# Giving GpSimd a fifth of the subtractions of a mixture-of-experts stage, and loading its first tiles later

## The chip, the cores and the metric

The kernel runs on one core of a Trainium2 chip, as one launch. The metric is the device time of that launch in microseconds (us), the median of repeated runs. Engines are named as in the profile: PE (TensorE matmuls) with PEld (its weight loads), ACT (ScalarE), DVE (VectorE), POOL (GpSimd), SP (SyncE, which here issues DMAs).

## The reference

The whole computation is two transformer blocks on 512 tokens of width 1024, in float32. The change concerns only the last feed-forward layer, a mixture of 8 experts over 256 tokens, two experts for each token:

```python
def swiglu(u, wg, wu, wd):
    return (jax.nn.silu(u @ wg) * (u @ wu)) @ wd

def moe_swiglu(u, w_router, wg, wu, wd):
    ...
    logits = (xf @ w_router).astype(F32)
    vals, idx = lax.top_k(logits, TOP_K_EXPERTS)
    w = jax.nn.softmax(vals, axis=-1)
    gate = jnp.sum(jax.nn.one_hot(idx, N_EXPERTS, dtype=F32) * w[..., None], axis=1)
    y = jnp.zeros_like(xf)
    for e in range(N_EXPERTS):
        y = y + gate[:, e:e + 1].astype(xf.dtype) * swiglu(xf, wg[e], wu[e], wd[e])
```

For each expert the gate and up matrices are 1024 x 3584 and the down matrix is 3584 x 1024.

## The kernel before

Everything ahead of the experts is a sequence of stages that the change leaves alone. `router_stage` picks two experts for each token. `seat_stage` gathers up to 128 tokens for each expert into `route.seated` with matmuls. `moe_stage` then computes the experts one after another. A second pass through both stages stands under a condition (an expert with over 128 tokens) and does not run here.

PE multiplies in the type fp32r, so each float32 operand is split in two: `hi`, its leading part, and `lo`, the rest. A product takes three matmul passes: x_hi w_hi, x_lo w_hi, x_hi w_lo. `moe_stage` streams the weights in **units** of 128 rows. An expert has 92: first 64 **up** units of 896 columns, in 4 groups of 16 (8 gate units, then 8 lift units, for a quarter of the hidden columns), then 28 **down** units of 1024 columns. For each unit u:

- SP loads its tile (mostly two units, 896 KB or 1 MB) into one of 6 raw slots. Three slots are the tensor `raw_ring`, two lie in `H`, one in the constants' level masks (`const`). A slot is loaded anew once the last unit of its old tile has been subtracted (`parted`).
- ACT copies the unit to `weights_hi` (L3321, counter `cut`). There are 4 buffers, so it waits until PE has used unit u-4.
- DVE computes `weights_lo` = raw - hi for the whole width (L3360, counter `parted`).
- PE waits for `parted` and does 6 matmuls (L3297), then counts `used`.

Between units each engine has other work at fixed places, in program order. In each group, at u % 16 == 11 ACT applies Silu to the gate rows and copies the turned rows to `hidden_hi` (L3329, L3336); at u % 16 == 3 of the next group DVE multiplies the rows (L3370), and at u % 16 == 12 it subtracts for `hidden_lo` (L3377), each as two instructions with one input in PSUM. PE transposes rows at u % 16 == 6 (L3256). The output of the expert before is copied at u = 3 and scattered and added from u = 5 to 16 (L3268, L3354).

At an expert's start ACT splits the seated tokens into `expert_x_hi` (L3316) after its last cut of the expert before, and POOL subtracts for `expert_x_lo` (L3243, 1024 columns), its only instruction in an expert. PE waits for it before unit 0.

`seat_stage` also loads the first 4 tiles of expert 0 (`MOE_EARLY`): they go to the three slots of `raw_ring` and to the masks, which that stage does not use. `moe_stage` starts with tile 4.

Of the kernel before, what the change touches and what calls it, by code (L numbers as in the profile page):

```python
# [2968 lines left out]
MOE_SLOTS, MOE_EARLY, MOE_GROUPS = 6, 4, 4  # L2969


class Raw:


    def __init__(self, core, st, route, turn):
        masks = CONST_AT["level0_0"][0]
        assert CONST_AT[f"level{LEVELS - 1}_1"][1] - masks == 2 * D
        in_H = st.H[:].rearrange("p k t -> p (k t)").rearrange("p (s n) -> p s n", s=2)
        self.at = [*(route.raw_ring[:, i] for i in range(MOE_SLOTS - 3)), st.const[:, masks:masks + 2 * D], in_H[:, 0], in_H[:, 1]]
        self.landed = [core.counter(f"moe_raw{s}_landed_{turn}", True) for s in range(MOE_SLOTS)]  # L2980
        self.w_up = [st.A[n][0].rearrange("e (k p) n -> p e k n", p=P) for n in ("moe_w_gate_2", "moe_w_up_2")]

    def load_up(self, sp, e, t):

        wide = FE // MOE_GROUPS
        g, m, k0 = t // DC, t % DC // 4, t % 4 * 2
        src = self.w_up[m][:, ds(e, 1), k0:k0 + 2, g * wide:(g + 1) * wide]
        at = self.at[t % MOE_SLOTS][:, 0:2 * wide].rearrange("p (k n) -> p k n", n=wide)
        sp.dma_start(at, src.rearrange("p e k n -> p (e k) n")).then_inc(self.landed[t % MOE_SLOTS].sem, 16)
# [159 lines left out]
def moe_stage(core, st, route, turn):  # L3149
# [27 lines left out]
    width_of = lambda u: WIDE if u < UP else D  # L3177

    with ExitStack() as ctx, core.engines_block() as block:
        raw_tiles = Raw(core, st, route, turn)  # L3180
# [16 lines left out]
        names = ("cut", "parted", "used", "x_cut", "x_ready", "gated", "rows_ready", "turned", "h_cut", "h_ready",  # L3197
                 "act_y_copied", "dve_y_copied", "scattered", "y_added")
        (cut, parted, used, x_cut, x_ready, gated, rows_ready, turned, h_cut, h_ready,
         act_y_copied, dve_y_copied, scattered, y_added) = (core.counter("moe_" + n) for n in names)  # L3200
# [358 lines left out]
```

## Time and profile before

| | |
|---|---|
| median of 3 runs | 3990.3 us (3982.96 to 3992.85) |
| the profiled execution's own time | 3990.3 us |
| its span, first to last instruction | 3988.3 us |
| PE, PEld busy over the span | 85%, 66% |
| DVE, ACT, POOL busy over the span | 63%, 37%, 9% |
| mean granted PE clock, as a share of full speed | 0.903 |
| the expert stage, first cut to the end of the last subtraction | 2938 to 3952 us |

The expert stage is the last quarter of the span; the shares over the whole span mix it with stages that have other limits, so the stage is read by itself. A timeline row gives the start, the duration, engine, line, operation, tile written <- tiles read, and in brackets the idle time of that engine before it and what ended it. Rows marked xN merge N instructions that follow one another.

### The profile page before, as it was taken

What the parts mean: (1) busy time and instruction counts of PE and PEld (TensorE: products, weight loads), DVE (VectorE), ACT (ScalarE), POOL (GpSimd) and SP (SyncE); (2) the same over time, 40 slices, a digit from 0 to 9 for tenths busy, and PEclk for the clock granted to TensorE, in tenths of its full rate; (3) what the DMA queues carried; (4) which work ended last, traced back from release to release, by engine and by line L of the source; (5) the groups of instructions that cost most, each with busy time, mean ns of one, the idle gap of its engine ahead of it and who ended that gap; (6) DMA issues with size and microseconds to landing.
All of it is one profiled execution on the core that took longest, in us unless ns stands there. A gap on an engine that the chain in (4) does not pass through costs nothing. (4 is left out here: it accounts for less than half of the span.)

```text
span 3988.3 us, 67458 instructions
## 1 busy us (share of the span) xinstructions
PE 3379.2 (85%) x25980; PEld 2632.9 (66%) x25980; DVE 2523.6 (63%) x4138; ACT 1478.8 (37%) x2693; POOL 346.1 (9%) x338
## 2 busy tenths in 40 slices
PE   5897876999778798779866798778689999999997
PEld 2644555874365687668764687665568888888886
DVE  2436657889666445669346351146458888888887
ACT  1123312110202665311011200214257777777775
POOL 0000003442100221021000020000000000000000
PEclk8998987999888899989986899865789999999998
DMA  7310012328222000168520495120159999999995
GB/s 307 95 56 1 1 42 79 95 92 256 79 88 60 3 5 4 36 223 277 192 89 7 143 320 175 68 87 3 43 211 356 338 355 343 350 351 344 346 348 205
DMA packets 296869, 645.55 MB, mean 162 GB/s; under 512 B 24989, under 2 KB 155145, under 8 KB 296521
## 3 DMA queue, kind: packets, MB, share of 16 engines
q1 hardware_dynamic: 272889, 556.32, 39.8%
q0 software_dynamic: 23040, 83.90, 6.1%
q8 instruction: 158, 2.59, 0.3%
q10 hardware_dynamic: 720, 2.23, 0.1%
q14 instruction: 62, 0.51, 0.0%
HBM read 641.34 MB, written 1.05 MB: 161 GB/s over the span
## 5 line engine op out<-in xcount | busy, mean ns | idle before, releaser
L3360 DVE TENSOR_TENSOR weights_lo<-raw_ring,weights_hi 128x896 fp32r<-128x896 f32 (+1 forms) x376 | 425.6, 1157 | 77.2 <-ACT weights_hi L3321 66.7
L3321 ACT ACTIVATE weights_hi<-raw_ring 128x896 fp32r<-128x896 f32 (+1 forms) x376 | 364.2, 985 | 122.3 <-PE bank_pair L3297 122.1
L323 PE MATMUL bank_pair<-H,ring_up 128*128 128x256 f32 x1408 | 311.0, 383 | 25.4 <-DMA ring_up<-in_ffn_w_gate 9.2
L3297 PE MATMUL bank_pair<-weights_hi,expert_x_hi 128*128 128x512 f32 (+1 forms) x1024 | 306.4, 380 | 21.9 <-DVE weights_lo L3360 21.9
L323 PEld LDWEIGHTS bank_pair<-H,ring_up 128*128 128x128 f32 x1408 | 269.1, 192 | 66.9 <-DVE conv L1760 11.0
L3297 PE MATMUL bank_pair<-weights_lo,expert_x_hi 128*128 128x512 f32 (+1 forms) x1024 | 294.2, 368 | 0.0
L3297 PE MATMUL bank_pair<-weights_hi,expert_x_lo 128*128 128x512 f32 (+1 forms) x1024 | 294.1, 368 | 0.0
L323 PE MATMUL bank_pair<-x_hi,ring_hi_in 128*128 128x512 f32 (+1 forms) x576 | 210.5, 365 | 94.7 <-DVE ring_lo_in L298 82.0
L3360 DVE TENSOR_TENSOR weights_lo<-H,weights_hi 128x896 fp32r<-128x896 f32 (+1 forms) x240 | 263.7, 1132 | 32.3 <-ACT weights_hi L3321 26.0
L3321 ACT ACTIVATE weights_hi<-H 128x896 fp32r<-128x896 f32 (+1 forms) x240 | 235.2, 993 | 77.9 <-PE bank_pair L3297 77.9
L323 PE MATMUL bank_pair<-ffn_h,ring_down 128*128 128x512 f32 (+1 forms) x704 | 232.2, 492 | 24.1 <-DMA ring_down<-in_ffn_w_down 19.9
L3297 PEld LDWEIGHTS bank_pair<-weights_hi,expert_x_hi 128*128 128x128 f32 x1024 | 181.7, 188 | 59.7 <-DVE weights_lo L3360 32.1
L323 PEld LDWEIGHTS bank_pair<-ffn_h,ring_down 128*128 128x128 f32 x704 | 134.8, 193 | 121.2 <-issue 88.1
L323 PE MATMUL bank_pair<-x_lo,ring_hi_in 128*128 128x512 f32 (+1 forms) x576 | 206.5, 358 | 0.0
L323 PE MATMUL bank_pair<-x_hi,ring_lo_in 128*128 128x512 f32 (+1 forms) x576 | 206.2, 358 | 0.0
L3297 PEld LDWEIGHTS bank_pair<-weights_hi,expert_x_lo 128*128 128x128 f32 x1024 | 186.7, 188 | 24.4
L3297 PEld LDWEIGHTS bank_pair<-weights_lo,expert_x_hi 128*128 128x128 f32 x1024 | 186.1, 188 | 24.7
L323 PEld LDWEIGHTS bank_pair<-x_hi,ring_hi_in 128*128 128x128 f32 x576 | 114.1, 198 | 117.6 <-DVE ring_lo_in L298 85.0
L1760 DVE SCALAR_TENSOR_TENSOR conv<-bank_pair,taps,conv 128x189 f32<-128x189 f32 (+2 forms) x352 | 151.0, 431 | 24.8 <-ACT conv L1791 13.1
L579 DVE SCALAR_TENSOR_TENSOR mod_sums_ada<-mod_ring_ada,act,mod_sums_ada 128x512 f32 (+1 forms) x192 | 144.1, 751 | 21.0 <-DMA mod_ring_ada<-in_w_ada 15.1
L323 PE MATMUL bank_pair<-x_hi,ring_hi_up 128*128 128x512 f32 x352 | 138.1, 392 | 19.8 <-DVE x_lo L355 19.8
L3297 PE MATMUL bank_pair<-weights_hi,hidden_hi 128*128 128x512 f32 x448 | 138.9, 391 | 0.0
(628 smaller groups left out, 6636.5 us busy)
## 6 DMA issues: line engine op xcount, KB each, us to landing
raw_ring<-in_moe_w_gate SPq DMA_DIRECT2D x72, 896.0 KB, 6.6
raw_ring<-in_moe_w_up SPq DMA_DIRECT2D x64, 896.0 KB, 6.3
ring_up<-in_ffn_w_up SPq DMA_DIRECT2D x110, 512.0 KB, 4.1
mod_ring_ada<-in_w_ada POOLq DMA_DIRECT2D x96, 512.0 KB, 6.5
raw_ring<-in_moe_w_down SPq DMA_DIRECT2D x48, 1024.0 KB, 7.0
H<-in_moe_w_up SPq DMA_DIRECT2D x48, 896.0 KB, 7.1
H<-in_moe_w_down SPq DMA_DIRECT2D x32, 1024.0 KB, 7.3
H<-in_moe_w_gate SPq DMA_DIRECT2D x32, 896.0 KB, 6.3
```

The costliest lines, as they stand in the source:

```text
L323: ins = self.core.nc.tensor.matmul(self.banks[o][:, 0:moving.shape[1]], lhs, moving, start=(s == self.first[o] and k == 0 and i == 0), sto ...
L579: self.core.nc.vector.scalar_tensor_tensor(at, self.ring[:, s, k % self.PART], self.st.act[:, k, c:c + 1], at, ALU.mult, ALU.add).then_inc ...
L1760: ins = nc.vector.scalar_tensor_tensor(yg[:, rows[0], rows[1]], xg[:, from_[0], from_[1]], taps[:, o, w:w + 1], yg[:, rows[0], rows[1]], A ...
L3297: ins = nc.tensor.matmul(banks[half][:, 0:b - a], x, w[:, a:b], start=start and i == 0, stop=stop and i == 2)
L3321: nc.scalar.activation(hi[:, u % CUTS, 0:n].bitcast(F32R), raw_part(u), ACT.Copy).then_inc(cut.sem, 1)
L3360: nc.vector.tensor_tensor(lo[:, u % CUTS, 0:n].bitcast(F32R), raw_part(u)[:, 0:n], hi[:, u % CUTS, 0:n], ALU.subtract).then_inc(parted.sem, 1)
```

## The change

1. The subtraction of a unit is divided by columns: DVE takes columns 0 to 703 of an up unit and 0 to 799 of a down unit; POOL takes the other 192 or 224. `parted` becomes two counters, `dve_parted` and `pool_parted`.
2. PE waits for both counters ahead of a unit. SP waits for both ahead of a tile, with an increment of a counter that nobody reads (`sp_passed`) between the two waits.
3. `seat_stage` loads nothing any more. SP loads all tiles of expert 0 in `moe_stage`, as one loop over 8 experts in place of a first round and a loop over 7. `raw_ring` is allocated in `moe_stage`.
4. The slots have another order: the masks are slot 5 and the halves of `H` are slots 3 and 4.

```diff
-        raw = Raw(core, st, route, turn)
-
-        @block.sync
-        def _(sp):
-            for t in range(MOE_EARLY):
-                raw.load_up(sp, 0, t)
...
+    dve_columns = lambda u: 704 if u < UP else 800
...
+        raw = [*(raw_ring[:, i] for i in range(SLOTS - 3)), raw_in_H[:, 0], raw_in_H[:, 1], st.const[:, masks:masks + 2 * D]]
...
         def _(sp):
-            def body(e, first):
-                for t in range(MOE_EARLY if first else 0, TILES):
-                    wait_parted(sp, e if t >= SLOTS else e - 1, units_of[t - SLOTS][-1])
+            with sp.Fori(0, EXPERTS) as e:
+                for t in range(TILES):
+                    u = units_of[t - SLOTS][-1]
+                    wait_pool_parted(sp, e if t >= SLOTS else e - 1, u)
+                    sp.sem_inc(sp_passed.sem, 1)
+                    wait_dve_parted(sp, e if t >= SLOTS else e - 1, u)
...
         def _(pool):
+            pool.sem_inc(pool_parted.sem, UNITS)
             with pool.Fori(0, EXPERTS) as e:
...
                 nc.gpsimd.tensor_tensor(x_lo[:].bitcast(F32R), seated, x_hi[:], ALU.subtract).then_inc(x_ready.sem, 1)
+                for u in range(UNITS):
+                    pool.wait_ge(cut.sem, cut.at(e * UNITS + u + 1))
+                    wait_used(pool, e if u >= CUTS else e - 1, (u - CUTS) % UNITS)
+                    at = slice(dve_columns(u), width_of(u))
+                    nc.gpsimd.tensor_tensor(lo[:, u % CUTS, at].bitcast(F32R), raw_part(u)[:, at], hi[:, u % CUTS, at], ALU.subtract).then_inc(pool_parted.sem, 1)
...
-                    wait_parted(pe, e, u)
+                    wait_pool_parted(pe, e, u)
+                    wait_dve_parted(pe, e, u)
...
             def body(e, first):
                 for u in range(UNITS):
-                    n = width_of(u)
+                    n = dve_columns(u)
                     dve.wait_ge(cut.sem, cut.at(e * UNITS + u + 1))
-                    nc.vector.tensor_tensor(lo[:, u % CUTS, 0:n].bitcast(F32R), raw_part(u)[:, 0:n], hi[:, u % CUTS, 0:n], ALU.subtract).then_inc(parted.sem, 1)
+                    nc.vector.tensor_tensor(lo[:, u % CUTS, 0:n].bitcast(F32R), raw_part(u)[:, 0:n], hi[:, u % CUTS, 0:n], ALU.subtract).then_inc(dve_parted.sem, 1)
```

## Rows read from the trace of the kernel before

**Rows 1.** Windows: length, busy time of each engine, PE clock, DMA share, GB/s.

```profile
2895.50:2908.00 12.50, 7.16 (x21) 4.91 (x22) 10.32 (x38) 0.00 (x0) 0.00 (x0) 0.51 0.77 294
2938.50:2945.20 6.70, 3.33 (x9) 2.97 (x10) 5.63 (x4) 3.74 (x5) 2.28 (x1) 0.50 0.89 301
2945.30:3953.00 1007.70, 992.19 (x4736) 847.98 (x4736) 889.89 (x895) 774.56 (x875) 16.80 (x7) 1.00 0.94 344
```

**Rows 2.** Waits from 2960 to 3940 us: total us, times, longest.

```profile
ACT weights_hi L3321 <- PE bank_pair L3297: 225.8, 585, 1.1
...
PE bank_pair L3297 <- DVE weights_lo L3360: 15.1, 31, 0.6
```

**Rows 3.** Timeline, unit pace: ACT cuts in the up and down phases.

```profile
3352.43 0.96 ACT L3321 ACTIVATE weights_hi<-raw_ring 128x896 fp32r<-128x896 f32 x1 [0.28 <-PE bank_pair L3297]
3353.67 0.96 ACT L3321 ACTIVATE weights_hi<-raw_ring 128x896 fp32r<-128x896 f32 x1 [0.29 <-PE bank_pair L3297]
...
3410.29 1.06 ACT L3321 ACTIVATE weights_hi<-H 128x1024 fp32r<-128x1024 f32 x1 [0.30 <-PE bank_pair L3297]
3411.65 1.07 ACT L3321 ACTIVATE weights_hi<-H 128x1024 fp32r<-128x1024 f32 x1 [0.29 <-PE bank_pair L3297]
```

**Rows 4.** Timeline of the end of a group of 16 units.

```profile
3358.23 1.81 ACT L3321 ACTIVATE weights_hi<-raw_ring 128x896 fp32r<-128x896 f32 x2
...
3359.23 1.09 DVE L3360 TENSOR_TENSOR weights_lo<-raw_ring,weights_hi 128x896 fp32r<-128x896 f32 x1 [1.48 <-ACT weights_hi L3321]
...
3360.24 1.15 DVE L3377 TENSOR_TENSOR hidden_lo<-bank_pair,hidden_hi 128x512 fp32r<-128x512 f32 x2
...
3361.30 1.08 DVE L3360 TENSOR_TENSOR weights_lo<-raw_ring,weights_hi 128x896 fp32r<-128x896 f32 x1
...
3362.44 0.68 PE L3297 MATMUL bank_pair<-weights_hi,expert_x_hi 128*128 128x512 f32 x2 [0.58 <-DVE weights_lo L3360]
```

**Rows 5.** Timeline of an expert's end and the next one's start; one DVE subtraction.

```profile
3317.80 1.77 ACT L3321 ACTIVATE weights_hi<-raw_ring 128x896 fp32r<-128x896 f32 x2
...
3318.07 2.40 POOL L3243 TENSOR_TENSOR expert_x_lo<-seated,expert_x_hi 128x1024 fp32r<-128x1024 f32 x1 [124.37 <-ACT expert_x_hi L3316]
...
3321.47 0.68 PE L3297 MATMUL bank_pair<-weights_hi,expert_x_hi 128*128 128x512 f32 x2 [0.19 <-DVE weights_lo L3360]
...
L3360 DVE TENSOR_TENSOR weights_lo<-raw_ring,weights_hi x1: 2651/2651/2651, 3318.8 to 3318.8; 128x896 fp32r<-128x896 f32 x1
```

**Rows 6.** Norm stage at 1061 us: POOL and DVE side by side; ns min/median/max.

```profile
L901 POOL TENSOR_TENSOR norm_work<-Y x2: 1029/1256/1483, 1061.5 to 1062.5; 128x512 f32<-128x512 f32 x2
...
L873 DVE TENSOR_TENSOR norm_work<-Y x4: 677/1102/1578, 1061.5 to 1065.1; 128x512 f32<-128x512 f32 x4
```

**Rows 7.** Groups of POOL by shape: 1024 and 256 columns.

```profile
L3243 POOL TENSOR_TENSOR expert_x_lo<-seated,expert_x_hi 128x1024 fp32r<-128x1024 f32 x8 | 19.2, 2394 | 943.8 <-ACT expert_x_hi L3316 943.8
...
L2296 POOL TENSOR_TENSOR kappa<-rw_k,kappa 128x256 f32<-128x256 f32 x16 | 11.7, 730 | 1.3
```

**Rows 8.** Group of DVE by shape: the 1024-column subtraction.

```profile
L3360 DVE TENSOR_TENSOR weights_lo<-H,weights_hi 128x1024 fp32r<-128x1024 f32 x78 | 91.8, 1219 | 1.9
```

**Rows 9.** Start of the expert stage; time to landing of its first DMA.

```profile
2938.14 3.45 ACT L3321 ACTIVATE weights_hi<-raw_ring 128x896 fp32r<-128x896 f32 x4
...
2941.88 1.09 PE L3297 MATMUL bank_pair<-weights_hi,expert_x_hi 128*128 128x512 f32 x2 [6.34 <-DVE weights_lo L3360]
...
L2989 SPq DMA_DIRECT2D H<-in_moe_w_up x1: 368/368/368, 2937.1 to 2937.1; - x1
...
DMA to landing us min/median/max: 5.0/5.0/5.0
```

**Rows 10.** First tile of the fifth expert: landing, and ACT's first use.

```profile
L2989 SPq DMA_DIRECT2D raw_ring<-in_moe_w_gate x1: 389/389/389, 3436.7 to 3436.7; - x1
...
DMA to landing us min/median/max: 6.5/6.5/6.5
...
3444.30 1.77 ACT L3321 ACTIVATE weights_hi<-raw_ring 128x896 fp32r<-128x896 f32 x2
```

More of the change, by code:

```diff
@@ L2966, in _ @@
                     nc.scalar.activation(dst[:, :, 0:N_CMP], bank[:, 0:KV_HEADS * N_CMP].rearrange("p (g n) -> p g n", g=KV_HEADS), ACT.Copy)
[L2969 to L2989, printed above, removed]
 class Route:
@@ L3146, in _, with moe_stage @@
                 stored.count(nc.scalar.activation(route.seated[:, g * 4:(g + 1) * 4, k], core.bank(n % 4).rearrange("p (e s) -> p e s", e=4), ACT.Copy))
-def moe_stage(core, st, route, turn):
+def moe_stage(core, st, route):
     nc, A = core.nc, st.A
-    GROUPS = MOE_GROUPS
+    GROUPS = 4
     WIDE = FE // GROUPS
@@ L3177, in moe_stage @@
     width_of = lambda u: WIDE if u < UP else D
+    dve_columns = lambda u: 704 if u < UP else 800
     with ExitStack() as ctx, core.engines_block() as block:
-        raw_tiles = Raw(core, st, route, turn)
-        raw, landed = raw_tiles.at, raw_tiles.landed
+        raw_ring = core.sb("raw_ring", [P, SLOTS - 3, 2 * D], ctx=ctx)
+        raw_in_H = st.H[:].rearrange("p k t -> p (k t)").rearrange("p (s n) -> p s n", s=2)
+        masks = CONST_AT["level0_0"][0]
+        assert CONST_AT[f"level{LEVELS - 1}_1"][1] - masks == 2 * D
+        raw = [*(raw_ring[:, i] for i in range(SLOTS - 3)), raw_in_H[:, 0], raw_in_H[:, 1], st.const[:, masks:masks + 2 * D]]
         hi, lo = (core.sb(f"weights_{n}", [P, CUTS, D], ctx=ctx) for n in ("hi", "lo"))
@@ L3196, in like @@
             return bank[half][:, 0:b - a].rearrange("p (c t) -> p c t", c=rows[half].shape[1])
[L3197 to L3200, printed above, removed]
+        landed = [core.counter(f"moe_raw{s}_landed") for s in range(SLOTS)]
+        names = ("cut", "dve_parted", "pool_parted", "used", "x_cut", "x_ready", "gated", "rows_ready", "turned", "h_cut", "h_ready",
+                 "act_y_copied", "dve_y_copied", "scattered", "y_added", "sp_passed")
+        (cut, dve_parted, pool_parted, used, x_cut, x_ready, gated, rows_ready, turned, h_cut, h_ready,
+         act_y_copied, dve_y_copied, scattered, y_added, sp_passed) = (core.counter("moe_" + n) for n in names)
         GATE, LIFT = (core.bank(0), core.bank(1)), (core.bank(2), core.bank(3))
         TURN, DOWN = (core.bank(4), core.bank(5)), (core.bank(6), core.bank(7))
+        w_up = [A[n][0].rearrange("e (k p) n -> p e k n", p=P) for n in ("moe_w_gate_2", "moe_w_up_2")]
         w_down = A["moe_w_down_2"][0].rearrange("e (k p) n -> p e k n", p=P)
@@ L3207, in raw_part, with wait_dve_parted, wait_pool_parted @@
             return raw[t % SLOTS][:, j * width_of(u):(j + 1) * width_of(u)]
-        def wait_parted(eng, e, u):
-            eng.wait_ge(parted.sem, parted.at(UNITS + e * UNITS + u + 1))
+        def wait_dve_parted(eng, e, u):
+            eng.wait_ge(dve_parted.sem, dve_parted.at(UNITS + e * UNITS + u + 1))
+        def wait_pool_parted(eng, e, u):
+            eng.wait_ge(pool_parted.sem, pool_parted.at(UNITS + e * UNITS + u + 1))
         def wait_used(eng, e, u):
@@ L3232, in body @@
                         src = w_down[:, ds(e, 1), c:c + n, :]
-                        at = raw[t % SLOTS][:, 0:n * D].rearrange("p (k n) -> p k n", n=D)
-                        sp.dma_start(at, src.rearrange("p e k n -> p (e k) n")).then_inc(landed[t % SLOTS].sem, 16)
-            rounds(sp, EXPERTS, body)
+                        at = at[:, 0:n * D]
+                    sp.dma_start(at.rearrange("p (k n) -> p k n", n=src.shape[3]), src.rearrange("p e k n -> p (e k) n")).then_inc(landed[t % SLOTS].sem, 16)
         @block.gpsimd
         def _(pool):
+            pool.sem_inc(pool_parted.sem, UNITS)
             with pool.Fori(0, EXPERTS) as e:
@@ L3385, in moe_stage @@
             c.n += 16 * LAPS * EXPERTS
-        for c, n in ((cut, UNITS * EXPERTS), (parted, UNITS * (EXPERTS + 1)), (used, UNITS * (EXPERTS + 1)),
+        for c, n in ((cut, UNITS * EXPERTS), (dve_parted, UNITS * (EXPERTS + 1)), (pool_parted, UNITS * (EXPERTS + 1)), (used, UNITS * (EXPERTS + 1)),
                      (x_cut, EXPERTS), (x_ready, EXPERTS), (gated, GROUPS * EXPERTS), (rows_ready, GROUPS * EXPERTS), (turned, 1 + GROUPS * EXPERTS),
                      (h_cut, GROUPS * EXPERTS), (h_ready, 1 + GROUPS * EXPERTS), (act_y_copied, EXPERTS), (dve_y_copied, EXPERTS),
+                     (sp_passed, EXPERTS * TILES),
                      (scattered, 4 * EXPERTS), (y_added, 4 * (EXPERTS + 1))):
```

14 lines of the change are left out of this document (8 added, 6 removed).

## The prediction

> **What bounds the kernel now.** I read the windows of the expert stage first. From 2945 to 3953 us PE is busy 992 of 1008 us at the granted clock 1.00, DVE 890, ACT 775, the DMA engines 0.94 of the time, POOL 17 us [rows 1]. Four numbers near full don't say which sets the pace; the list of waits does. ACT waits for PE to free a buffer 585 times, and PE waits for DVE's subtraction 31 times, 15.1 us in all [rows 2]. So PE sets the pace, and DVE, though 88% busy, costs about 15 us. The timeline gives PE's pace through ACT, which starts each cut as PE frees a buffer: 1.24 us for an up unit, 1.36 us for a down unit [rows 3]. An expert takes 126.5 us (first cuts at 3317.80 and 3444.30) [rows 5, 10].
>
> The 31 waits are of two kinds, by count 3 x 8 group ends and 7 expert starts. At a group's end ACT's extra work delays the cut of unit 28; DVE subtracts it, does `hidden_lo` (1.15 us) and only then unit 29, from 3361.30 to 3362.38, and PE goes on at 3362.44 after 0.58 us idle [rows 4]. At an expert's start POOL's `expert_x_lo` runs from 3318.07 to 3320.47, DVE's first subtraction, begun at 3318.8, takes 2.65 us instead of 1.09 and ends at 3321.42, and PE starts 0.05 us later, after 0.19 us idle [rows 4, 5].
>
> **POOL and DVE exclude each other here.** That 2.65 us is the row on which most depends. DVE ended 0.95 us after POOL did, whenever it had started. The norm stage shows the same for 512 columns: POOL's first instruction took 1.03 us, DVE's longest 1.58 against 0.68 alone, that is 0.55 after POOL, and POOL's next took 1.48 instead of 1.03, since it waited in turn [rows 6]. The waiting instruction has done its start-up by then (0.68 - 0.55 = 0.13 us, and 1.09 - 0.95 = 0.14). `hidden_lo` and the row products read PSUM with one operand; I take it that they don't join this queue.
>
> **The change, part by part.**
>
> *The shared resource per unit.* DVE holds it 0.95 us for 896 columns and 0.55 for 512, 1.04 ns a column: 0.75 us for 704 and 0.85 for 800 [rows 5, 6]. POOL alone takes 2.39 us for 1024 columns and 0.73 for 256, 2.17 ns a column [rows 7], so 0.59 us for 192 and 0.66 for 224. Its hidden start-up is between 0.10 (1.48 - 0.55 = 0.93 against 1.03, [rows 6]) and 0.17 (what the line through rows 7 leaves at no columns), so it holds 0.42 to 0.49 and 0.49 to 0.56 us. Together: 1.17 to 1.24 us for an up unit against PE's 1.24, and 1.34 to 1.41 for a down unit against PE's 1.36. I take 1.20 and 1.36. Before, DVE alone needed 1.09 and 1.22 [rows 4, 8], less where they overlap. The change thus lowers DVE's instruction and raises what a unit needs of the shared resource; it fits under PE, but with nothing to spare in the down phase. A backlog made there stays.
>
> *Group ends, 24 of them.* Unit 28 is ready after 0.14 + 0.75 + 0.45 = 1.34 us instead of 1.09, which is covered by the wait for unit 29. DVE reaches unit 29 about 0.2 us earlier, at 3361.1. By then POOL holds the resource for unit 30 (cut at about 3360.9: units 28 and 29 are cut by 3358.23 + 1.81 = 3360.04, the next one 0.85 later [rows 4]) until about 3361.55; DVE then ends at 3362.30 instead of 3362.38. Gain 0.08 x 24 = 1.9 us. Bounds: a gain of 0.2 each if POOL is not in between, a loss of 0.25 if it comes in ahead once more: -5 to +6 us.
>
> *Expert starts, 7 of them.* POOL now has unit 91 ahead of `expert_x_lo`. Unit 91 is cut some 0.85 us before ACT's first cut of the next expert (only `expert_x_hi` lies between), at about 3316.95 [rows 5]. Without a backlog both engines are through with it at 3316.95 + 0.15 + 1.36 = 3318.45; `expert_x_lo` holds from 3318.6 for 2.25 us to 3320.85, DVE's unit 0 ends at 3321.6 and POOL's, new, at 3322.05. PE starts 0.6 us later than at 3321.47. If unit 91 is late by 1 us, or DVE's unit 0 gets in ahead of `expert_x_lo` (they ask at nearly the same time), POOL's unit 0 comes behind DVE's unit 1: 3321.9 + 0.75 + 0.45 = 3323.1, 1.6 us late. With both it is 2.2 us. All of PE's matmuls are queued behind its new wait for POOL, and PE has no slack afterwards to win this back, so it lengthens the run. I take 1.5, near the second case, since the down phase clears no backlog: 7 x 1.5 = 10.5 us; bounds 4 and 15.
>
> *Down phase.* DVE comes into it behind, and the row products (two instructions, as long as `hidden_lo`, 1.15 us) stand at unit 67. POOL can only fill some 0.9 us of such a pause, as it runs out of cut units. Followed unit by unit with 1.34 us, unit 68 is 0.25 us late for PE and unit 77 up to 0.15 us. I take 0.35 x 8 = 2.8 us; bounds 0 and 8.
>
> *The early tiles.* SP issued four tiles in `seat_stage` (the DMA engines were busy 0.77 of 2895 to 2908 us); nothing waited for them there, so taking them out gives nothing. Before, the first cut was at 2938.14 and PE started at 2941.88 [rows 9]. Now the first tile is issued at 2937.1 and lands 5.0 us later, as the first one issued there does [rows 9]: 2942.1. Cut 0.96, DVE 0.89, POOL 0.45 more: PE starts at 2944.4, 2.5 us later. Later tiles come faster than PE uses them at first. PE ran its first microseconds at the granted clock 0.50 [rows 1], the level of 1.2 GHz; idle 2.5 us longer it may stay there a little longer, and each microsecond there does half the work of one at full clock: 0.8 us more (0 to 2). Sum 3.3, bounds 2.5 and 4.5.
>
> *SP's two waits.* The counter increment and the second wait delay a tile by a fraction of an issue (0.37 us, [rows 9]); a backlog of subtractions delays it by up to 1 us. The thinnest place is an expert's first tile: issued at 3436.7, landed at 3443.2, used at 3444.30 [rows 10], a margin of 1.1 us, and behind it the cut may be 2 us late, because `expert_x_lo` holds DVE up anyway. What is queued behind SP's waits is the next tiles alone. Costed at nothing; without that cover a backlog of 1 us would cost up to 1 us an expert. The order of the slots moves no byte: nothing. POOL's loop over 92 units has no other work queued behind it but `expert_x_lo`, counted above.
>
> *The sum.* 3.3 + 10.5 + 2.8 - 1.9 = 14.7 us. The profiled execution took 3990.3 us (span 3988.3), which is also the median: 4005.0 us, 0.37% slower.
>
> **A rule that says more.** The trace has the waiting DVE instruction finish 0.95 us after POOL and not 1.09, so its start-up was not held [rows 4, 5]. The Trainium skill, "SBUF — State Buffer", section "Who interferes with whom", says that the shared pair of ports goes to whichever of DVE and GpSimd issues first, for the whole instruction. Taken at its word, with whole durations, this gives the fourth rival's time; with the held times the rule and the rows agree, and the sum stands.
>
> **The rivals.**
>
> *1. They run side by side when POOL's instruction is this short (8%).* Then units 28 and 29 are each 0.2 us earlier, 24 x 0.4 = 9.6 us, expert starts gain 0.1 each, and the early tiles cost 3.3: 3990.3 - 9.6 - 0.7 + 3.3 = 3983 us, not slower. It decides only if POOL's hold is nought; rows 5 and 6 are against it, though both are for POOL instructions of 512 columns and more.
>
> *2. Everything but the start is hidden (14%).* The pauses of PE (transposes, scatters) clear the backlog, and unit 91 is never late: 3.3 + 7 x 0.3 - 1.9 = 3.5: about 3994 us. For it: 1.20 is under 1.24. Against: DVE has 1.15 us pauses in every group.
>
> *3. The resource is the bound (17%).* If POOL holds over 0.49 us for 192 columns or 0.51 for 224, each unit is longer than PE's. At 0.05 us over for an up unit and 0.08 for a down unit an expert takes 64 x 0.05 + 28 x 0.08 = 5.4 us more, 43 us in all with the pauses of PE giving some back: 4020 to 4060 us.
>
> *4. Whole instructions exclude each other (4%).* 0.89 + 0.59 = 1.48 for an up unit, 0.99 + 0.66 = 1.65 for a down unit: 64 x 0.24 + 28 x 0.29 = 23.5 us an expert, 188 us in all: 4178 us. Against it: the 0.95 and 0.55 us above.
>
> *5. Late tiles (2%).* The margin of 1.1 us falls below nothing at 7 starts and the cover is gone: some 7 us on top, 4012 us.
>
> **How the numbers follow.** The forecast has 55%, with a range of its own of 3996 to 4016 us. A measurement here tells about 0.3%, 12 us, from no change: above 4002.3 is slower. Two thirds of the forecast (37%), rivals 3, 4 and 5 (23%) lie there: 60%. The rest of the forecast, rival 2 and most of rival 1 are within it: 36%. Faster keeps 4%, for a rival 1 that also takes away the remaining group waits. For 8 in 10 the range runs from 3988 (rival 1 left out) to 4035 (half of rival 3 and rival 4 left out).
>
> **What would show it.** POOL subtractions of 0.56 to 0.66 us alone and about 1.3 when they wait; DVE's at 0.89 alone and up to 1.35 behind POOL; PE waiting for POOL by name; PE's first matmul near 2944.4; first cuts of successive experts some 128.2 us apart, against 126.5; units of 1.24 and 1.36 us in between. It is wrong if the distance stays at 126.5 (rival 2), falls (rival 1), or if the units themselves lengthen (rivals 3 and 4), and if ACT waits for a DMA at an expert's start (rival 5).

## The result and the profile after

The changed kernel takes 4046.1 us (median of 4 runs, 4043.88 to 4056.86) against 3991.6 us for the kernel before in the same comparison. The ratio is 1.0144, 95% interval 1.0118 to 1.0170: slower, and above the predicted range. The profiled execution of after took 4066.35 us. Its expert stage begins 20.8 us later than that of before (first cut 2958.9 against 2938.1); 4.4 us of this belong to the change, the rest to stages that the change leaves alone and that vary between executions. So the expert stage is read by itself, and mainly one number of it: the distance from an expert's first cut to the next one's, a mean over experts 2 to 7. It is 126.79 us before and 134.83 after, 8.0 us more where the terms of the sum gave 1.6 (1.5 + 0.35 - 3 x 0.08).

The windows of after: the first from 7.2 us behind the stage's first cut to its end, as in [rows 1], the second behind one expert's start:

```profile
2966.10:4029.00 1062.90, 1012.37 (x4726) 849.56 (x4725) 932.58 (x894) 773.80 (x874) 801.81 (x739) 0.98 0.91 328
3499.90:3504.00 4.10, 4.09 (x11) 3.62 (x12) 0.50 (x2) 0.95 (x1) 1.86 (x4) 0.50 0.99 372
```

PE's busy time is longer than in [rows 1] and the clock no longer 1.00; POOL went from 17 to 802 us. The second row shows why the clock fell: 4.1 us at 0.50, the level of 1.2 GHz, behind an idle PE. The waits of the stage, against [rows 2]:

```profile
ACT weights_hi L3312 <- PE bank_pair L3288: 263.7, 573, 5.8
...
PE bank_pair L3288 <- POOL weights_lo L3233: 39.5, 7, 6.8
POOL expert_x_lo L3228 <- issue: 32.6, 7, 5.3
...
ACT weights_hi L3312 <- DMA raw_ring<-in_moe_w_gate: 20.4, 13, 3.5
...
PE bank_pair L3288 <- DVE weights_lo L3351: 7.3, 25, 0.5
```

PE's waits for DVE halved, from 15.1 to 7.3 us. In their place stand 7 waits for POOL of 5.6 us each: the seven expert starts. POOL itself, ahead of each `expert_x_lo`, stood 32.6 us in all waiting for nothing that the profile shows ("issue"), and ACT waited 13 times for a tile.

Between the starts the units kept their pace. ACT's cuts in both phases, POOL's subtraction of an up unit alone, and DVE's of a down unit, against [rows 3]:

```profile
3395.60 0.95 ACT L3312 ACTIVATE weights_hi<-raw_ring 128x896 fp32r<-128x896 f32 x1 [0.28 <-PE bank_pair L3288]
3396.84 0.96 ACT L3312 ACTIVATE weights_hi<-raw_ring 128x896 fp32r<-128x896 f32 x1 [0.29 <-PE bank_pair L3288]
...
3485.01 1.06 ACT L3312 ACTIVATE weights_hi<-H 128x1024 fp32r<-128x1024 f32 x1 [0.30 <-PE bank_pair L3288]
3486.37 1.07 ACT L3312 ACTIVATE weights_hi<-H 128x1024 fp32r<-128x1024 f32 x1 [0.30 <-PE bank_pair L3288]
...
3390.51 0.60 POOL L3233 TENSOR_TENSOR weights_lo<-H,weights_hi 128x192 fp32r<-128x192 f32 x1 [0.64 <-ACT weights_hi L3312]
...
3485.60 1.45 DVE L3351 TENSOR_TENSOR weights_lo<-raw_ring,weights_hi 128x800 fp32r<-128x800 f32 x1
```

1.24 us and 1.36 us, as before. POOL's 192 columns take 0.60 us alone (0.59 predicted), DVE's 800 take 1.45 us beside POOL (up to 1.35 predicted).

The timeline of the boundary where the fifth expert begins, against [rows 5] and [rows 10]:

```profile
3480.64 0.33 SPq L3219 DMA_DIRECT2D const<-in_moe_w_down  x1
3485.81 2.90 SPq L3219 DMA_DIRECT2D raw_ring<-in_moe_w_gate  x3
...
3488.70 1.05 ACT L3307 ACTIVATE expert_x_hi<-seated 128x1024 fp32r x1
...
3488.96 1.40 POOL L3233 TENSOR_TENSOR weights_lo<-const,weights_hi 128x224 fp32r<-128x224 f32 x1
...
3490.99 1.80 ACT L3312 ACTIVATE weights_hi<-raw_ring 128x896 fp32r<-128x896 f32 x2 [1.24 <-DMA raw_ring<-in_moe_w_gate]
...
3494.51 1.79 ACT L3312 ACTIVATE weights_hi<-raw_ring 128x896 fp32r<-128x896 f32 x2 [1.72 <-DMA raw_ring<-in_moe_w_gate]
3495.49 3.84 DVE L3351 TENSOR_TENSOR weights_lo<-raw_ring,weights_hi 128x704 fp32r<-128x704 f32 x2 [1.78 <-ACT weights_hi L3312]
3495.63 2.94 POOL L3228 TENSOR_TENSOR expert_x_lo<-seated,expert_x_hi 128x1024 fp32r<-128x1024 f32 x1 [5.28 <-issue]
...
3498.54 2.88 POOL L3233 TENSOR_TENSOR weights_lo<-raw_ring,weights_hi 128x192 fp32r<-128x192 f32 x4
...
3499.91 1.11 PE L3288 MATMUL bank_pair<-weights_hi,expert_x_hi 128*128 128x512 f32 x2 [6.77 <-POOL weights_lo L3233]
```

POOL ends unit 91 at 3490.36. `expert_x_hi` has been ready since 3489.75, and yet `expert_x_lo` starts at 3495.63: 5.28 us in which POOL waits for no one. PE needs it, and POOL's part of unit 0 behind it, and starts at 3499.91 after 6.77 us idle (5.3 to 5.9 at the other six starts, 0.19 in [rows 5]). SP has a hole too: no tile is issued between 3480.64 and 3485.81, and so the first tiles of the new expert land late; ACT waits 1.24 and 1.72 us for them. In both streams the hole stands exactly behind the jump from the end of the loop's body to its start. Measured from the end of the branch instruction to the next instruction:

| engine | kernel before | after, at its 7 jumps |
|---|---|---|
| POOL | 0.11 us | 5.4 to 6.3 us |
| SP | 0.20 us | 4.0 to 4.3 us |
| DVE, ACT | 0.2 us | 0.2 us |

The page's list of DMA queues has a row that answers to it, the queue that brings instructions. First after, then before:

```profile
q14 instruction: 136, 1.11, 0.1%
```

```profile
q14 instruction: 62, 0.51, 0.0%
```

74 packets more in an execution. When they come says more than how many. From 3300 to 3900 us, a stretch that holds no stage but this one, the kernel before has no packet of this queue, and after has 46:

```profile
q14 instruction: 46, 0.38, 0.2%
```

Most come in bursts behind SP's and POOL's jumps: 7 lie between 3481 and 3500 us, around the boundary shown above. Instructions are being loaded again.

### The profile page after: what moved, and what is told of

Read it like the earlier page. It is cut to its first block and busy times, and to the rows that moved or that the text cites. A ratio compares the mean times of both kernels' runs of the same rounds, so it can differ in the third digit from the quotient of the medians.

```text
span 4064.4 us, 70956 instructions
## 1 busy us (share of the span) xinstructions
PE 3414.1 (84%) x25980; PEld 2642.5 (65%) x25980; DVE 2568.1 (63%) x4138; ACT 1478.0 (36%) x2693; POOL 1137.4 (28%) x1074
## 3 DMA queue, kind: packets, MB, share of 16 engines
HBM read 641.34 MB, written 1.05 MB: 158 GB/s over the span
## 5 line engine op out<-in xcount | busy, mean ns | idle before, releaser
L3351 DVE TENSOR_TENSOR weights_lo<-raw_ring,weights_hi 128x704 fp32r<-128x704 f32 (+1 forms) x376 | 438.7, 1205 | 101.2 <-ACT weights_hi L3312 100.5
L3233 POOL TENSOR_TENSOR weights_lo<-raw_ring,weights_hi 128x192 fp32r<-128x192 f32 (+1 forms) x376 | 399.8, 1075 | 135.5 <-ACT weights_hi L3312 108.7
L3288 PE MATMUL bank_pair<-weights_hi,expert_x_hi 128*128 128x512 f32 (+1 forms) x1024 | 314.9, 389 | 57.2 <-POOL weights_lo L3233 49.6
L3351 DVE TENSOR_TENSOR weights_lo<-H,weights_hi 128x704 fp32r<-128x704 f32 (+1 forms) x240 | 283.1, 1216 | 26.5 <-ACT weights_hi L3312 26.2
L3233 POOL TENSOR_TENSOR weights_lo<-H,weights_hi 128x192 fp32r<-128x192 f32 (+1 forms) x240 | 259.1, 1089 | 68.1 <-ACT weights_hi L3312 57.0
L901 POOL TENSOR_TENSOR norm_work<-X 128x512 f32<-128x512 f32 x7 | 8.2, 1170 | 771.1 <-SPq L196 771.1
```

Source lines behind the costliest of these rows:

```text
L901: nc.gpsimd.tensor_tensor(work[0][:, q], jobs[0].x(q), jobs[0].x(q), ALU.mult).then_inc(pool_squared.sem, 1)
L3233: nc.gpsimd.tensor_tensor(lo[:, u % CUTS, at].bitcast(F32R), raw_part(u)[:, at], hi[:, u % CUTS, at], ALU.subtract).then_inc(pool_parted.s ...
L3288: ins = nc.tensor.matmul(banks[half][:, 0:b - a], x, w[:, a:b], start=start and i == 0, stop=stop and i == 2)
L3351: nc.vector.tensor_tensor(lo[:, u % CUTS, 0:n].bitcast(F32R), raw_part(u)[:, 0:n], hi[:, u % CUTS, 0:n], ALU.subtract).then_inc(dve_parted ...
```

## The experiments

What had to be told apart: (a) how much of the 8.0 us is this reloading, (b) what makes a loop reload, its length or something else, (c) whether POOL and DVE exclude each other with their held times, as predicted, (d) what the start and the group ends are worth. The loop's body, in instructions of one expert:

| | POOL | SP | DVE | ACT |
|---|---|---|---|---|
| before | 6 | 176 | 224 | 219 |
| after | 282 | 269 | 224 | 251 |

All distances below are of one profiled execution each, as the mean of six; the ratios are of 4 to 10 runs beside the kernel before. They are not the quotients of the two pooled medians, which differ from them by up to 0.2% (`short_both`: ratio 1.0044, medians 4021.9 and 3997.0 us, quotient 1.0062). A difference of 0.2% or less between two kernels is therefore read from the trace and not from the ratios.

### 1. Shorter loops: POOL alone, then POOL and SP

`short_pool` drops POOL's wait for the buffer of `weights_lo`, which PE's use has cleared anyway once ACT has cut the unit (190 instructions left). `short_both` also merges SP's waits at ten pairs of tiles (249 left).

```diff
                     pool.wait_ge(cut.sem, cut.at(e * UNITS + u + 1))
-                    wait_used(pool, e if u >= CUTS else e - 1, (u - CUTS) % UNITS)
...
+        AHEAD = (8, 11, 14, 17, 20, 23, 26, 29, 32, 35)
...
-                    sp.sem_inc(sp_passed.sem, 1)
-                    wait_dve_parted(sp, e if t >= SLOTS else e - 1, u)
+                    if t - 1 not in AHEAD:
+                        sp.sem_inc(sp_passed.sem, 1)
+                        wait_dve_parted(sp, e if t >= SLOTS else e - 1, units_of[t + 1 - SLOTS][-1] if t in AHEAD else u)
```

> The changed kernel without POOL's wait for `used` ahead of each subtraction (the wait for `cut` implies it); POOL does the same 93 subtractions an expert with about 190 instead of 282 instructions in its loop's body. Theory A (a loop's branch back stalls an engine for about 5.5 us when the body is longer than the engine holds, somewhere between 251 and 271 instructions by the traces so far): the gap behind POOL's branch falls from 5.4 to 6.3 us to about 0.1, and the first cuts of successive experts stand 128 to 130 us apart instead of 134.8; the time falls from 4046 to 4005 to 4015 us. Theory B (POOL and DVE together are the bound because they exclude each other): the waits taken away hold already, so nothing changes: 4046 us and 134.8. Theory C (the cost lies in SP's late tiles): POOL's gap may go, but the distance stays above 132.

> As short_pool, and SP's body is cut from 271 to 251 instructions too: at 10 of the 48 tiles SP waits for DVE's subtraction of one tile further on and leaves out the wait and the increment at the next tile. Theory A: the gap behind SP's branch falls from 4.1 us to 0.2, ACT no longer waits for a tile at an expert's start, and the distance of experts is 127.5 to 129 us, the time 4000 to 4008 us, what my prediction of 4005 had costed without any branch. Theory B: 134.8 and 4046. Theory C: only this kernel, and not short_pool, falls below 132.

Measured: `short_pool` 1.0045 [1.0029, 1.0061], distance 129.08 us; POOL's hole is gone (0.0 us), SP's is still there (4.0 to 5.0). `short_both` 1.0044 [1.0027, 1.0062], distance 129.02; both are gone. The same boundary in `short_both`:

```profile
3473.15 1.05 ACT L3309 ACTIVATE expert_x_hi<-seated 128x1024 fp32r x1
...
3473.38 1.42 POOL L3235 TENSOR_TENSOR weights_lo<-const,weights_hi 128x224 fp32r<-128x224 f32 x1
...
3474.09 1.78 ACT L3314 ACTIVATE weights_hi<-raw_ring 128x896 fp32r<-128x896 f32 x2
...
3474.76 3.15 POOL L3231 TENSOR_TENSOR expert_x_lo<-seated,expert_x_hi 128x1024 fp32r<-128x1024 f32 x1
...
3475.57 5.49 DVE L3353 TENSOR_TENSOR weights_lo<-raw_ring,weights_hi 128x704 fp32r<-128x704 f32 x3
...
3479.23 0.67 PE L3290 MATMUL bank_pair<-weights_hi,expert_x_hi 128*128 128x512 f32 x2 [1.66 <-POOL weights_lo L3235]
```

`expert_x_lo` starts 0.67 us after ACT's first cut, PE 5.14 us after it (3479.23 - 3474.09); before it was 3.67 us (3321.47 - 3317.80, [rows 5]). The difference is 1.47 us. So POOL's reloading cost 5.8 us an expert, 134.83 - 129.08, and SP's hole nothing that can be told while it stood (129.08 against 129.02): in `short_pool` ACT waits 18.9 us in all for tiles, but PE has to wait for `expert_x_lo` and the subtractions behind it for as long anyway. Of the 5.8 us, 4.0 are PE's longer wait (5.64 us in the mean against 1.67). The other 1.8 are longer matmuls. From the second expert's first matmul to the eighth's, six experts, PE's busy time is 767.94 us in after and 756.71 in `short_both`, 1.87 an expert more. First after, then `short_both`:

```profile
3094.33:3903.34 809.01, 767.94 (x3577) 645.06 (x3577) 708.38 (x679) 584.24 (x660) 605.77 (x559) 0.98 0.91 327
```

```profile
3092.29:3866.36 774.07, 756.71 (x3576) 633.86 (x3577) 724.39 (x679) 584.38 (x660) 627.31 (x559) 1.00 0.91 341
```

The count of matmuls is the same and the clock is not: in `short_both` it stays at 1.00 at every one of these starts, in after it is 0.50 for 3.4 to 6.8 us around each.

### 2. Length or place: the same loops moved

A length limit would have to lie between 249 and 269. The other theory is that instructions lie in blocks with fixed borders, that two blocks are held, and that a body which touches a third must be loaded anew at each jump. `pad_dve` makes DVE's loop of the kernel before longer than any of these, by a second, needless wait at the 64 up units (288 instructions). `shift_both` takes the loops of after as they are and moves them, by 40 instructions ahead of them on POOL and on SP. `pad_dve_moved` does it the other way round: the loop of `pad_dve`, 212 instructions further on.

```diff
                     dve.wait_ge(cut.sem, cut.at(e * UNITS + u + 1))
+                    if u < 64:
+                        dve.wait_ge(cut.sem, cut.at(e * UNITS + u + 1))
```

```diff
+            for _ in range(40):
+                sp.sem_inc(shift.sem, 1)
...
+            for _ in range(40):
+                pool.sem_inc(shift.sem, 1)
```

```diff
+            for _ in range(212):
+                dve.sem_inc(shift.sem, 1)
```

> The kernel before with each of DVE's waits for `cut` in the up phase written twice: 64 more instructions that wait for nothing new, 288 instead of 224 in the body of DVE's loop, no more data and no POOL. Theory A: the gap behind DVE's branch grows from 0.23 to 4 to 6 us at each of 6 branches back and stops PE for most of it, 25 to 45 us in all: 4015 to 4035 us. Theory B: within 2 us of the kernel before, as nothing more is shared. Theory C: the same as B.

> The changed kernel with 40 increments of a counter that nobody waits for put ahead of the loop on POOL and on SP, in the stage before, where both are idle. The bodies stay 282 and 271 instructions long; only where they lie in each engine's program moves by about 42. So far bodies of 282 (POOL), 265 and 271 (SP) stalled at their branch back, but 288 (DVE) did not, so length alone (theory A) does not explain it. Theory D: an engine holds two pages of 256 instructions, and a body that touches a third is fetched again at each branch; by the positions of all loops seen, the pages would begin at about 812 and 1068, and the bodies, which began at 791 and 811, now begin at 833 and 856 and touch two. Then the gaps fall to 0.1 and 0.2 us, experts stand 129 us apart and the time is as short_both, 4005 to 4020 us. Theory A: gaps 5.4 and 4.1 us, 134.8 us, 4046 us as before.

> pad_dve (the kernel before with 64 idle waits in DVE's loop, 288 instructions, which had no gap) with 212 idle increments put ahead on DVE in the stage before, in a 26 us pause of DVE. Theory D: the body now runs from about 3867 to 4154 and holds two page starts, so the same body stalls: gap 4 to 6 us at 6 branches, 20 to 40 us in all. Theory A' (DVE does not stall at all, only POOL and SP do): gap 0.25 us and the time of pad_dve, 1.002 of the kernel before.

Measured: `pad_dve` 1.0018 [1.0002, 1.0034], distance 127.15, DVE's jump 0.25 us. A body of 288 instructions is not reloaded, so length alone is not the cause. `shift_both`: 1.0043 [1.0030, 1.0056], distance 128.86; bodies of 282 and 272 instructions, no shorter than in after, and jumps of 0.19 and 0.20 us (0.24 and 0.26 the first time). Forty instructions of nothing ahead of the loops win back 1.0%. `pad_dve_moved`: 1.0060 [1.0041, 1.0080], distance 129.55, and DVE's jump takes 5.5 to 5.8 us. Its boundary:

```profile
3465.53 1.78 ACT L3325 ACTIVATE weights_hi<-raw_ring 128x896 fp32r<-128x896 f32 x2
...
3465.80 2.41 POOL L3247 TENSOR_TENSOR expert_x_lo<-seated,expert_x_hi 128x1024 fp32r<-128x1024 f32 x1 [127.36 <-ACT expert_x_hi L3320]
...
3470.83 4.10 DVE L3366 TENSOR_TENSOR weights_lo<-raw_ring,weights_hi 128x896 fp32r<-128x896 f32 x4 [4.89 <-ACT weights_hi L3325]
...
3471.97 0.67 PE L3301 MATMUL bank_pair<-weights_hi,expert_x_hi 128*128 128x512 f32 x2 [2.95 <-DVE weights_lo L3366]
```

DVE has the cut of the next unit from 3466.5 on and starts at 3470.83, 4.89 us idle behind what the profile calls a wait for ACT; PE starts at 3471.97 after 2.95 us. At six starts PE waits 2.7 to 3.0 us; at the seventh, where DVE's first expert, which has its own code, runs on into the loop without a jump, it waits 0.26. The distances behind a jump are 131.43, 129.77, 129.73, 129.70 and 129.43 us, against 127.14 in `pad_dve`: 2.9 us a jump (the sixth distance, 127.21, has no jump ahead of it and lowers the mean to 129.55). That is less than POOL's 5.8. PE waits 2.8 us here and not 5.6, since only unit 0 is queued behind the hole, and the clock fell at only one of the six starts, the one with 131.43.

The places, counted in each engine's compiled program, fit blocks of 256 instructions whose borders lie at the same remainder in all three programs. SP's 269 and 272 are also what the traces count between two jumps (the expectations have 271 for both):

| loop | body at | borders in it | blocks | reloaded |
|---|---|---|---|---|
| after, POOL | 791 to 1072 | 814, 1070 | 3 | yes |
| after and short_pool, SP | 813 to 1081 | 814, 1070 | 3 | yes |
| short_pool, POOL | 791 to 980 | 814 | 2 | no |
| short_both, SP | 813 to 1061 | 814 | 2 | no |
| shift_both, POOL | 833 to 1114 | 1070 | 2 | no |
| shift_both, SP | 855 to 1126 | 1070 | 2 | no |
| pad_dve, DVE | 3655 to 3942 | 3886 | 2 | no |
| pad_dve_moved, DVE | 3867 to 4154 | 3886, 4142 | 3 | yes |

The borders are inferred (46 to 48 more than a multiple of 256 fits: 45 would leave SP's loop of after in two blocks, 49 POOL's), the yes and no are measured. The packets of the instruction queue agree: 136 in after, 101 in `short_pool`, 65 in `short_both`, 68 in `shift_both`, 63 in `pad_dve`, 96 in `pad_dve_moved`. From 3300 to 3900 us there are 24 in `short_pool` and 24 in `pad_dve_moved`, and none in `short_both`, `shift_both` and `pad_dve`. That is 5 packets of 8.2 KB for each jump that reloads. The Trainium skill, "Runtime: NRT & Kernel Launch", section "Instruction fetch mechanics", states the rule: an engine other than PE holds two blocks of 256 instructions, and a taken branch to a target outside them forces a fetch. The runs agree on both numbers; the price of 4.0 to 6.3 us is theirs.

### 3. How much POOL's share costs: 16, 192 and 384 columns

`narrow` and `wide_b` are `short_both` with another division of the columns.

```diff
-    dve_columns = lambda u: 704 if u < UP else 800
+    dve_columns = lambda u: 880 if u < UP else 1008
```

```diff
-    dve_columns = lambda u: 704 if u < UP else 800
+    dve_columns = lambda u: 512 if u < UP else 592
```

> short_both (no stalls behind branches) with POOL given 16 columns of each unit instead of 192 or 224, and DVE 880 or 1008. All waits and instructions are the same; only the time that POOL holds the shared access shrinks, by my estimate from 0.45 to 0.05 us, while DVE's grows from 0.75 to 0.93. If mutual exclusion makes the 2.2 us an expert that short_both still costs (129.0 against 126.8), this takes most of it back: 127 to 127.8 us. If it is the order of POOL's work (unit 91 and then unit 0 around the 1024-column subtraction) it stays above 128.5.

> short_both with the split moved the other way: POOL subtracts 384 or 432 columns, DVE 512 or 592. If the two exclude each other for the times that I worked out (2.17 ns a column for POOL, 1.04 for DVE plus nothing), a unit needs 0.83 + 0.55 = 1.38 us in the up phase and 0.94 + 0.63 = 1.57 in the down phase, more than PE's 1.24 and 1.36, so the shared access sets the pace: 64 x 1.38 + 28 x 1.57 + 2.2 = 134.5 us an expert, at least 133, and about 4055 us. If they run side by side, each alone needs 0.97 or less, and the expert stays at 127 to 129 us.

`narrow`: 1.0011 [0.9992, 1.0029], distance 127.13, within the range expected for exclusion; the order of POOL's work alone would have left it above 128.5. `wide_b`: 1.0328 [1.0303, 1.0353], distance 142.20. Two units of a down phase in `wide_b`:

```profile
3638.26 1.31 POOL L3235 TENSOR_TENSOR weights_lo<-raw_ring,weights_hi 128x432 fp32r<-128x432 f32 x1 [0.30 <-ACT weights_hi L3314]
...
3639.87 1.31 POOL L3235 TENSOR_TENSOR weights_lo<-raw_ring,weights_hi 128x432 fp32r<-128x432 f32 x1 [0.30 <-ACT weights_hi L3314]
...
3643.36 1.70 DVE L3353 TENSOR_TENSOR weights_lo<-H,weights_hi 128x592 fp32r<-128x592 f32 x1
```

POOL's starts are 1.61 us apart, the median of the phase (1.43 in an up phase), and DVE's 592 columns take 1.70 us. By the held times of the prediction a unit needs 592 x 1.04 ns = 0.62 us for DVE and 432 x 2.17 ns = 0.94 us for POOL, which may hold up to 0.07 more: 1.56 to 1.63. Whole instructions, 0.62 + 0.14 and 0.94 + 0.17, would take 1.87 us. So the two exclude each other with their held times, and POOL's is at the upper bound taken. The same bound gives 1.39 us for a down unit of the change, where DVE's subtractions in after start 1.38 us apart (median of a down phase) and PE's units 1.36.

Where in an expert the time goes is seen from ACT's cuts. The mean over six experts of the time between the cuts of two units, as the difference to the kernel before (us):

| units | what lies there | short_both | after | narrow | wide_b | group_end |
|---|---|---|---|---|---|---|
| 0 to 4 | expert start | +1.46 | +5.52 | +0.30 | +1.93 | +0.01 |
| 4 to 12 | | -0.03 | +0.79 | 0.00 | +0.83 | -0.01 |
| 12 to 27 | | 0.00 | 0.00 | 0.00 | +0.41 | 0.00 |
| 27 to 34, 43 to 50, 59 to 66 | group ends | -0.91 | -1.05 | -0.08 | +0.40 | -1.13 |
| 34 to 43, 50 to 59 | row products | +0.84 | +0.93 | +0.12 | +5.04 | +0.14 |
| 66 to 74 | row products, down phase | +0.86 | +0.85 | 0.00 | +3.16 | +0.01 |
| 74 to 92 | | 0.00 | +1.00 | 0.00 | +3.63 | 0.00 |
| all | | +2.2 | +8.0 | +0.3 | +15.4 | -1.0 |

The row products are two DVE instructions, 1.15 us, in which POOL goes on only as far as units are cut. In `wide_b` the stretches around them hold 8.2 of its 15.4 us, but only about 3 of these are the products themselves (the one long step between cuts in each of the three stretches, 1.0 to 1.1 us above its neighbours); the rest is units that are all 0.19 to 0.25 us longer. The expectation of 134.5 us missed 142.2 by 7.7: 4.3 because the units took 1.43 and 1.61 us instead of 1.38 and 1.57 (64 x 0.05 + 28 x 0.04), and 3.4 by such pauses, which it did not have.

### 4. The start of the stage

`no_early` is the kernel before without the four early tiles (SP's loop then begins at tile 0). `short_early_b` is `short_both` with them.

```diff
-        @block.sync
-        def _(sp):
-            for t in range(MOE_EARLY):
-                raw.load_up(sp, 0, t)
...
-                for t in range(MOE_EARLY if first else 0, TILES):
+                for t in range(TILES):
```

> The kernel before with only the four early tile loads taken out; nothing is shared with POOL. As costed in the prediction: PE's first matmul of the expert stage comes 2.1 to 2.5 us later and the time is 2.5 to 4.5 us longer, too little to be told from no change. If the early loads are the cause: over 15 us.

> short_both with the four early tile loads put back in the stage before. As costed, PE's first matmul of the expert stage comes about 2.5 us earlier against the start of that stage, nothing else moves (129.0 us an expert), and the ratio to the kernel before falls from 1.0044 by under 0.001. If the early loads matter more than their start (a lead that PE keeps), it falls below 1.002.

The start in `no_early` (the expert's tokens are cut at 2946.23):

```profile
2946.23 1.06 ACT L3311 ACTIVATE expert_x_hi<-seated 128x1024 fp32r<-128x1024 f32 x1 [2.76 <-PEq L3242]
...
2950.99 1.79 ACT L3316 ACTIVATE weights_hi<-raw_ring 128x896 fp32r<-128x896 f32 x2 [3.70 <-DMA raw_ring<-in_moe_w_gate]
2951.97 2.09 DVE L3355 TENSOR_TENSOR weights_lo<-raw_ring,weights_hi 128x896 fp32r<-128x896 f32 x2 [6.17 <-ACT weights_hi L3316]
...
2953.21 1.08 PE L3292 MATMUL bank_pair<-weights_hi,expert_x_hi 128*128 128x512 f32 x2 [8.62 <-DVE weights_lo L3355]
```

The same rows of after, against [rows 9]:

```profile
2958.92 1.79 ACT L3312 ACTIVATE weights_hi<-raw_ring 128x896 fp32r<-128x896 f32 x2 [4.27 <-DMA raw_ring<-in_moe_w_gate]
...
2961.34 1.09 PE L3288 MATMUL bank_pair<-weights_hi,expert_x_hi 128*128 128x512 f32 x2 [9.39 <-POOL weights_lo L3233]
```

In both ACT waits for the first tile. In `no_early` PE starts 6.98 us after `expert_x_hi` begins, against 4.70 in before: 2.3 us later. The second expert's first cut, measured from the same point, is 2.9 us later (130.00 against 127.07), and with the division of the columns 3.9 us later (`short_both` 131.77, `short_early_b` 127.89). The ratios can't show it: 1.0001 [0.9987, 1.0014] for `no_early`, and 1.0062 [1.0037, 1.0086] for `short_early_b` beside 1.0044 [1.0027, 1.0062] for `short_both`. So the 3 to 4 us are seen in the trace only; no run showed them in the time.

### 5. Using what worked: half of one unit at each group end

The one place where dividing the work gained is the group end, -0.3 us each. `group_end` is the kernel before with POOL taking columns 448 to 895 of units 29, 45 and 61 alone, while DVE does `hidden_lo`, which reads PSUM with one operand.

```diff
+    SHARED, HALF = (29, 45, 61), 448
...
+                for u in SHARED:
+                    pool.wait_ge(cut.sem, cut.at(e * UNITS + u + 1))
+                    at = slice(HALF, WIDE)
+                    nc.gpsimd.tensor_tensor(lo[:, u % CUTS, at].bitcast(F32R), raw_part(u)[:, at], hi[:, u % CUTS, at], ALU.subtract).then_inc(halved.sem, 1)
...
-                    n = width_of(u)
+                    n = HALF if u in SHARED else width_of(u)
```

> The kernel before, with POOL helping only where PE waits for DVE: at units 29, 45 and 61 of each expert POOL subtracts 448 of the 896 columns while DVE does the hidden_lo subtraction, and DVE the other 448; everything else stays. If PE's wait there is DVE's 1.09 us behind hidden_lo, and POOL can work beside hidden_lo since that reads PSUM, PE goes on about 0.45 us earlier at each of 24 places: 126.8 to 125.5 us an expert, about 10 us or 0.25% less. If hidden_lo shares with POOL after all, POOL ends late and the time is the same or longer.

Measured: 0.9971 [0.9951, 0.9992], distance 125.81, 0.98 us less than before; over 8 experts 7.8 us, or 0.2%. A group end, against [rows 4]:

```profile
3496.71 1.81 ACT L3336 ACTIVATE weights_hi<-raw_ring 128x896 fp32r<-128x896 f32 x2
...
3497.71 1.09 DVE L3375 TENSOR_TENSOR weights_lo<-raw_ring,weights_hi 128x896 fp32r<-128x896 f32 x1 [1.48 <-ACT weights_hi L3336]
...
3498.60 1.24 POOL L3256 TENSOR_TENSOR weights_lo<-raw_ring,weights_hi 128x448 fp32r<-128x448 f32 x1 [39.65 <-ACT weights_hi L3336]
3498.72 1.15 DVE L3392 TENSOR_TENSOR hidden_lo<-bank_pair,hidden_hi 128x512 fp32r<-128x512 f32 x2
...
3499.79 0.61 DVE L3375 TENSOR_TENSOR weights_lo<-raw_ring,weights_hi 128x448 fp32r<-128x448 f32 x1
...
3500.54 0.67 PE L3312 MATMUL bank_pair<-weights_hi,expert_x_hi 128*128 128x512 f32 x2 [0.20 <-DVE weights_lo L3375]
```

POOL's 448 columns run from 3498.60 to 3499.84, beside `hidden_lo`, which is as long as in [rows 4] (1.15 us). DVE's half is done at 3500.40, 3.69 us after the cut of unit 28, against 4.15 before (3362.38 - 3358.23). PE's idle time fell from 0.58 to 0.20 us. The interval lies just below 1 and the distance is shorter at each of the experts, so the gain is real but small: 0.1% by the pooled medians (3992.0 and 3995.9 us), 0.2% by the trace, 0.3% by the ratio.

## Why the prediction was wrong

**The step that failed** is the last sentence on SP's waits: "POOL's loop over 92 units has no other work queued behind it but `expert_x_lo`, counted above." The loop's own jump was costed at nothing, and with it the code that it has to hold: 282 instructions instead of 6, in three blocks. It cost 5.8 us at each of 7 starts, 40.7 us, or 1.0% (1.0144 against 1.0043 when the same loops lie in two blocks). Nothing of this was in the rows of before, whose jumps all took 0.1 to 0.3 us, but the lengths of the loops could be counted, and the rule stood in the Trainium skill. Without this term the forecast of 4005.0 us, 0.37% slower, stands beside 0.44% [0.27, 0.62] for `short_both`, and 1.6 us an expert beside 2.2. In part that is luck: two terms below are off by 0.7 and 1.35 us an expert in opposite directions. (The forecast distance of 128.2 us also started from one expert's 126.5; the mean was 126.79.)

**Expert starts.** Predicted +1.5 us each, by unit 91 or DVE's unit 0 being in the way. Measured +1.46 without the reloading. In `short_both` unit 91 was late: POOL starts it at 3473.38, ends at 3474.80, and `expert_x_lo` waits for that.

**Group ends.** Predicted -0.08 each, with bounds of -0.2 and +0.25. Measured -0.30: mis-sized, beyond the bound. The step assumed that POOL would hold the shared resource for unit 30 when DVE comes to unit 29. DVE came first. The group end in after:

```profile
3538.64 1.81 ACT L3312 ACTIVATE weights_hi<-raw_ring 128x896 fp32r<-128x896 f32 x2
...
3540.46 1.15 DVE L3368 TENSOR_TENSOR hidden_lo<-bank_pair,hidden_hi 128x512 fp32r<-128x512 f32 x2
...
3541.52 0.88 DVE L3351 TENSOR_TENSOR weights_lo<-raw_ring,weights_hi 128x704 fp32r<-128x704 f32 x1
...
3542.46 0.30 PEld L3288 LDWEIGHTS bank_pair<-weights_hi,expert_x_hi 128*128 128x128 f32 x2 [0.23 <-DVE weights_lo L3351]
...
3541.51 1.35 POOL L3233 TENSOR_TENSOR weights_lo<-H,weights_hi 128x192 fp32r<-128x192 f32 x1
```

Both ask for it within 0.01 us. DVE's unit 29 takes 0.88 us, its time alone, and POOL's unit 30 takes 1.35 instead of 0.59. PE loads the weights of unit 29 3.8 us after the cut of unit 28, against 4.2 in [rows 4].

**Row products.** Predicted +0.35 an expert, at unit 67 alone. Measured +0.86 there, and +0.84 at units 35 and 51 together, for which the prediction has no term. The delay comes at once and is not won back, since PE sets the pace: in `short_both` the step to ACT's cut of unit 72, which waits for PE's unit 68, is 0.65 us longer than before, where the prediction found 0.25, and the steps to the cuts of units 40 and 56 are 0.44 and 0.40 longer. The 0.25 was followed with 1.34 us for a down unit, the lower end of the prediction's own 1.34 to 1.41; DVE's starts are 1.38 apart. The two mis-sized terms nearly cancel: -0.91 + 1.70 = +0.8, against -0.24 + 0.35 = +0.1.

**The units.** Right: 1.24 and 1.36 us between them, POOL 0.60 alone.

**The start.** 3.3 us predicted, 2.9 and 3.9 measured in the trace.

**SP's waits.** "Costed at nothing" holds for the waits, though not by the cover named: SP's 93 further instructions made its loop reload, the tiles came 4 us late, and PE did not feel it only because `expert_x_lo` was later still.

**The rivals.** 1 (side by side) is refuted by `narrow` and `wide_b`: the time grows with POOL's columns. 2 (only the start) by the +2.2 us an expert of `short_both`. 3 (the resource is the bound) gave a time that holds the measured one, 4020 to 4060 us, by a cause that is all but absent. Its condition is met in the down phase (1.38 us against PE's 1.36), but the units that ACT's cuts show stay at 1.24 and 1.36, except for 0.01 to 0.03 us each at units 68 to 73 of `short_both`. 4 (whole instructions exclude each other, the cited rule taken at its word) is refuted by units of 1.36 us, and by 1.61 in `wide_b`, where it gives 1.87; here the measurement decides. 5 (late tiles) happened and cost nothing.

What stays open: where exactly the blocks' borders come from, and why POOL's jump takes longer than SP's with as many packets.

## What to carry to other kernels

Ahead of moving work into a loop, count the instructions of its body, waits and increments included, on each engine: one of up to 256 lies in at most two blocks wherever it stands (none of 176 to 251 stalled here), a longer one (269 to 288) stalled at each jump or not by its place, and then 40 needless instructions ahead of it, or a wait less in each step, are worth more than the arithmetic. In a trace, look for idle time put down to nothing ("issue") at the first instruction of a loop, and compare the packets of the instruction queue. Where POOL and DVE take turns, give POOL pieces that run while DVE reads PSUM, and leave it out of the steady stretches.

## What was not expected of the hardware

- A jump back to code that is no longer held costs 5.4 to 6.3 us on POOL, 4.0 to 4.3 (5.0 in `short_pool`) on SP, and 5.5 to 5.8 on DVE, and moves 5 packets of 8.2 KB.
- Idle time behind a jump or a loop's end is not always such a reload. ACT stands 5.33 us behind the end of its loop in before and in after, but it starts at 3955.02 in before, as PE's last matmul of the stage ends at 3954.99: it waits for PE.
- PE's clock fell to 0.50 behind idle times of 5.3 to 6.8 us at the seven starts and stayed there for 3.4 to 6.8 us. Behind idle times of 1.7 us (`short_both`) it stayed at 1.00. Behind those of 2.7 to 3.0 us (`pad_dve_moved`) it fell once in six, for 3.4 us behind 2.88.
- A subtraction of 16 columns on POOL takes 0.21 us alone, one of 192 0.59 and one of 384 1.00.
